# Modulation sums as rows, and latent-head outputs by token in halves of the array

## What is computed

```python
silu_c = jax.nn.silu(c)
silu_cc = jax.nn.silu(c_ctx)
m_lat = (silu_c @ w_ada[layer] + b_ada[layer])[:, None, :]
m_ctx = silu_cc @ w_ada[layer] + b_ada[layer]
sh1, sc1, g1, sh2, sc2, g2 = jnp.split(m_lat, N_MOD, axis=-1)
csh1, csc1, cg1, csh2, csc2, cg2 = jnp.split(m_ctx, N_MOD, axis=-1)
u_lat = _modulate(_rmsnorm(x, norm1_g[layer]), sh1, sc1)
u_ctx = _modulate(_rmsnorm(ctx, norm1_g[layer]), csh1, csc1)
```

```python
scores = jnp.einsum("bnihd,bnjhd->bnhij", qc * jnp.exp(a - a_mid), kc * jnp.exp(a_mid - a))
scores = jnp.where(tril, scores, 0.0)
o_intra = jnp.einsum("bnhij,bnjhe->bnihe", scores, vc)
o_inter = jnp.einsum("bnihd,bnhde->bnihe", qc * jnp.exp(a), s_start)
o = o * lax.rsqrt(jnp.mean(o * o, axis=-1, keepdims=True) + EPS) * gain
return o.reshape(bb, l, HG_WIDTH) * jax.nn.silu(g)
```

## Time and profile before

| | before |
|---|---|
| median of the runs, us | 2680.01 |
| the profiled execution's own time, us | 2679.24 |
| its span, us | 2677.4 |
| TensorE busy, share of the span | 99% |
| VectorE, ScalarE, POOL busy | 68%, 49%, 11% |
| mean granted TensorE clock | 0.998 |
| share of TensorE in the chain that ended last | 94% |
| read from HBM | 564.73 MB, 212 GB/s |

### The profile page before, as it was taken

One profiled execution on the slowest core, in us unless ns is written; L12 is line 12 of the kernel. 1 busy time (PEld: TensorE's weight loads), 2 busy tenths in 40 slices (PEclk: granted clock), 3 DMA queues, 4 the chain that ended last, 5 costly groups with the idle time before them and its releaser, 6 DMA issues.

```text
span 2677.4 us, 42752 instructions
## 1 busy us (share of the span) xinstructions
PE 2642.8 (99%) x18168; PEld 2414.4 (90%) x18168; DVE 1833.4 (68%) x2189; ACT 1323.8 (49%) x1746; POOL 281.4 (11%) x255
## 2 busy tenths in 40 slices
PE   9999999999999999999999999999999999999998
PEld 8888976998998989988999999998898898998997
DVE  5555665798999777787678866676555675445555
ACT  5455553554443443466874345666454444443443
POOL 1232321010000000010010311110000000000011
PEclk9999999999999999999999999999999999999999
DMA  9545454577777777795566744445657775555553
GB/s 308 171 156 158 146 175 143 195 262 269 271 260 285 269 284 282 283 338 176 157 233 243 266 134 150 136 151 194 219 170 251 266 282 196 190 177 196 188 179 124
DMA packets 289117, 571.28 MB, mean 213 GB/s; under 512 B 9702, under 2 KB 32513, under 8 KB 288608
## 3 DMA queue, kind: packets, MB, share of 16 engines
q1 hardware_dynamic: 283376, 548.69, 60.2%
q0 software_dynamic: 5552, 19.87, 2.5%
HBM read 564.73 MB, written 3.27 MB: 212 GB/s over the span
## 4 chain that ended last, share of the span: by engine, by line
PE 94%; DVE 3%; ACT 3%; issue 1%; POOL 0%; ACTq 0%; DVEq 0%; POOLq 0%
PE p_gemm L2110 49%; PE p_gemm L2159 32%; PE p_gemm L2136 3%; DVE w_lo L1232 1%; ACT w_hi L691 1%; PE p_b L2183 1%; PE p_b L2313 1%; PE p_b L2344 1%; PE p_b L2508 1%; PE p_b L2517 1%; PE p_b L2572 1%; PE p_b L2406 1%; PE p_gemm L2129 0%; PE p_b L2220 0%; PE p_b L2327 0%
## 5 line engine op out<-in xcount | busy, mean ns | idle before, releaser
L1232 DVE TENSOR_TENSOR w_lo<-w_raw,w_hi 128x1024 fp32r<-128x1024 f32 (+2 forms) x872 | 1068.5, 1229 | 729.7 <-ACT w_hi L691 728.5
L691 ACT ACTIVATE w_hi<-w_raw 128x1024 fp32r<-128x1024 f32 (+2 forms) x872 | 898.8, 1033 | 1226.4 <-PE p_gemm L2110 690.8
L2110 PE MATMUL p_gemm<-h_hi,w_hi 128*128 128x256 f32 x2928 | 831.5, 284 | 4.6 <-DVE w_lo L1232 2.5
L2110 PE MATMUL p_gemm<-h_lo,w_hi 128*128 128x256 f32 x2928 | 822.6, 281 | 0.0
L2110 PE MATMUL p_gemm<-h_hi,w_lo 128*128 128x256 f32 x2928 | 822.5, 281 | 0.0
L2110 PEld LDWEIGHTS p_gemm<-h_hi,w_hi 128*128 128x128 f32 x2928 | 551.7, 188 | 13.2 <-issue 7.1
L2110 PEld LDWEIGHTS p_gemm<-h_lo,w_hi 128*128 128x128 f32 x2928 | 551.9, 188 | 0.4
L2110 PEld LDWEIGHTS p_gemm<-h_hi,w_lo 128*128 128x128 f32 x2928 | 551.7, 188 | 0.0
L2159 PE MATMUL p_gemm<-w_hi,a_hi 128*128 128x512 f32 (+1 forms) x1056 | 406.1, 385 | 0.1
L2159 PE MATMUL p_gemm<-w_hi,a_lo 128*128 128x512 f32 (+1 forms) x1056 | 404.4, 383 | 0.0
L2159 PE MATMUL p_gemm<-w_lo,a_hi 128*128 128x512 f32 (+1 forms) x1056 | 404.2, 383 | 0.0
(11 more groups left out here) (402 smaller groups left out, 2483.2 us busy)
## 6 DMA issues: line engine op xcount, KB each, us to landing
w_raw<-in_w_mlp SPq DMA_DIRECT2D x124, 1024.0 KB, 5.2
w_raw<-in_w_in SPq DMA_DIRECT2D x107, 1024.0 KB, 5.3
ada_w<-in_w_ada SPq DMA_DIRECT2D x96, 1024.0 KB, 5.5
w_raw<-in_w_up SPq DMA_DIRECT2D x64, 1024.0 KB, 7.5
w_raw<-in_w_down SPq DMA_DIRECT2D x64, 1024.0 KB, 8.2
w_raw<-in_w_out SPq DMA_DIRECT2D x32, 1024.0 KB, 5.1
w_raw<-in_w_in SPq DMA_DIRECT2D x36, 768.0 KB, 4.7
cmp_w<-in_phi_w POOLq DMA_DIRECT2D x2, 2048.0 KB, 19.1
```

The source lines that it names most:

```text
L691: act.activation(WH[:, s % 4, :, 0:n], RAW[:, s // 2, 2 * (s % 2):2 * (s % 2) + 2, 0:n], ACT.Copy)\
L1232: dve.tensor_tensor(WL[:, s % 4, :, 0:n], RAW[:, s // 2, 2 * (s % 2):2 * (s % 2) + 2, 0:n], WH[:, s % 4, :, 0:n].bitcast(F32), ALU.subtrac ...
L2110: ins = pe.matmul(dst, w[:, s % 4, kk, cols], x[:, k, :], start=k == 0 and m % 2 == 0 and i == 0, stop=k == KC - 1 and i == 2, skip_group_ ...
```

## The change

It changes three things, and moves some steps for room.

**Sums as rows.** After the last step ScalarE rounds the 512 summed columns to `ADAT` and VectorE writes the remainder. TensorE, now after unit 3 (`ADA_AT`), multiplies a selector with them: 32 weight columns, of which one is ones, so that the total lands as row `i` of `PADA[0:32]` and zeros are added to the other rows. Three times (blocks 33, 57, 75) VectorE copies the 32 rows (`MODR`), TensorE turns them by four small transposes, and VectorE adds the bias as before. The last four totals, those of g2, have a full array of ones as weights; their row comes out on all partitions at once and VectorE adds it to the bias row in `G2B`. `ADA_BLOCKS` begins at 16 and skips 55.

**Outputs by token.** Weights and moving operand of the output products change places, so that the output is 128 tokens by 128 channels, twice. The sum of squares is then taken by ScalarE's accumulator along the row, the scale is one number per token (`HRS`), VectorE multiplies it in (`lat_scale`), and TensorE turns the result back (`lat_turn`) for `lat_out`.

**Halves of the array.** The scores are eight products of 64 x 64 on the diagonal instead of four of 128 x 128, and the inter-chunk products have 64 weight columns; both write partitions 0 to 63 or 64 to 127.

```diff
-ADA_AT = 2
-ADA_BLOCKS = [*range(17, 48), *range(55, 62), 72, 73, *range(80, 88)]
+ADA_AT = 3
+ADA_BLOCKS = [*range(16, 48), *range(56, 62), 72, 73, *range(80, 88)]
-MOD_READS = (13, 16, 20, 24)
+ADA_G2 = 20
+MOD_READS = (8, 16, 20)
+MOD_AT = (B_MLP1 + 17, B_HY + 1, B_WOUT2 + 3)
+MOD_ROWS = (0, 16, 24)
-C_SCALE = (13, 15, 19, 22)
-C_TURN = (14, 15, 16, 17, 20, 21, 23, 24)
+C_ROOT = B_MLP1 + 24
+C_SCALE = (0, 5, 11, 18)
+C_TURN = (1, 3, 7, 9, 13, 16, 20, 23)
-U_SCALE = (6, 11, 19, 29)
-U_TURN = (9, 14, 20, 25, 30, 36, 41, 46)
+U_SCALE = (6, 11, 19, 33)
+U_TURN = (12, 14, 20, 28, 36, 44, 52, 54)
...
+            def ada_top(b):
...
+                act.wait_ge(S("ada_summed"), 2 * UPB * (i + 1))
+                if i < ADA_CTX:
+                    act.activation(ADAT[:, 2, :], CTXA[:, i % 2, :], ACT.Copy)
+                act.activation(ADAT[:, 0, :], ADA[:, 1, 3, :], ACT.Copy).then_inc(S("ada_hi"), 1)
...
             def lat_square(h):
                 act.wait_ge(S("hg_o"), h + 1)
-                act.activation(OSQ[:, :], PB[1][:, 0:T], ACT.Square).then_inc(S("hg_osq"), 1)
+                for tb in range(2):
+                    ins = act.activation(OSQ[:, P * tb:P * tb + P], PB[1][:, P * tb:P * tb + P], ACT.Square, accum_out=HSS[:, tb:tb + 1])
+                ins.then_inc(S("hg_osq"), 1)
...
+                act.activation(HRS, HSS, ACT.Ln, bias=prm("eps"), scale=1.0 / P).then_inc(S("hg_oln"), 1)
...
+            def ada_rest(b):
...
+                dve.wait_ge(S("ada_hi"), i + 1)
+                if i < ADA_CTX:
+                    dve.tensor_tensor(CTXL[:, i % 2, :], CTXA[:, i % 2, :], ADAT[:, 2, :].bitcast(F32), ALU.subtract)
+                dve.tensor_tensor(ADAT[:, 1, :], ADA[:, 1, 3, :], ADAT[:, 0, :].bitcast(F32), ALU.subtract).then_inc(S("ada_lo"), 1)
+
             def ada_step(b, s):
+                if s == 1:
+                    ada_rest(b)
...
+            def lat_scale(h):
+
+                dve.wait_ge(S("hg_ors"), h + 1)
+                for tb in range(2):
+                    ins = dve.tensor_scalar(ON[:, tb, :], PB[1][:, P * tb:P * tb + P], HRS[:, tb:tb + 1], None, ALU.mult)
+                ins.then_inc(S("hg_out"), 1)
...
+                        if s == 3 and h > 0:
+                            lat_scale(h - 1)
                         if s == 4:
                             lat_keys(h)
-                        if s == 3 and h > 0:
+                        if s == 5 and h > 0:
                             lat_out(h - 1)
...
+                if s == 2:
+                    lat_scale(HG - 1)
                 if s == 3:
                     lat_out(HG - 1)
                     gated(0)
...
             clamp_gate(1)
+            slot(B_WOUT2, None, 0)
+            ada_step(B_WOUT2, 0)
             gated(1)
+            slot(B_WOUT2, None, 1)
+            ada_step(B_WOUT2, 1)
             mixed_lo(3)
...
+                pe.wait_ge(S("ada_lo"), i + 1)
+                halves = (ADAT[:, 0, :], ADAT[:, 1, :])
+                if i >= ADA_G2:
+                    ps = bank(i % 2, "mod_ready", i - ADA_G2 + 4)
+                    for n, w in enumerate(halves):
+                        ins = pe.matmul(ps[:, :], SEL[:, 31:32].to_broadcast([P, P]), w, start=n == 0, stop=n == 1)
+                else:
+                    rows = [(i if i < ADA_CTX else i + 8, halves)]
+                    if i < ADA_CTX:
+                        rows.append((i + 8, (ADAT[:, 2, :], CTXL[:, i % 2, :])))
+                    for row, ws in rows:
+                        for n, w in enumerate(ws):
+                            ins = pe.matmul(PADA[0:32, :], SEL[:, 31 - row:63 - row], w, start=i == 0 and row == 0 and n == 0, stop=True,
+                                            skip_group_check=True)
+                ins.then_inc(S("ada_used"), 1)
+
+            def modulation_turn(part):
+
+                pe.wait_ge(S("mod_rows"), part + 1)
+                ps = bank(0, "mod_ready", part + 1)
                 for m in range(4):
...
+                    ins = pe.transpose(ps[:, 32 * m:32 * m + 32], MODR[part][:, P * m:P * m + P], IDN[0:32, 0:32])
+                ins.then_inc(S("mod_turned"), 1)
...
                 for z in range(2):
-                    for i in range(2):
-                        ts = slice(P * i, P * i + P)
-                        ins = pe.matmul(PB[1][:, T * z + P * i:T * z + P * i + P], KM[:, z, ts], QM[:, z, ts], start=True, stop=True)
+                    for n in range(NCH):
+                        ts = slice(CHUNK * n, CHUNK * n + CHUNK)
+                        ins = pe.matmul(PB[1][CHUNK * (n % 2):CHUNK * (n % 2) + CHUNK, T * z + CHUNK * n:T * z + CHUNK * n + CHUNK],
+                                        KM[:, z, ts], QM[:, z, ts], start=True, stop=True)
...
+                bank(1, "hg_out", 2 * h + 1)
                 for z in range(2):
                     for i in range(2):
...
+                        pe.matmul(PB[1][:, P * i:P * i + P], SCT[:, z, i, :], HVN[:, i, :], start=z == 0 and i == 0, stop=False,
+                                  skip_group_check=True)
+                for i in range(NCH):
+                    for z in range(2):
                         n = i if z == 0 else NCH - 1 - i
                         state = start_state(h)[:, z, :] if i == 0 else ST[:, z, i - 1, :]
...
+                        rows = slice(CHUNK * (n % 2), CHUNK * (n % 2) + CHUNK)
+                        cols = slice(P * (n // 2), P * (n // 2) + P)
+                        ins = pe.matmul(PB[1][rows, cols], QAQ[:, z, CHUNK * n:CHUNK * n + CHUNK], state, start=False, stop=True,
+                                        skip_group_check=True)
...
+            def lat_turn(h):
+
+                ps = bank(1, "hg_out", 2 * h + 2)
+                for tb in range(2):
+                    ins = pe.transpose(ps[:, P * tb:P * tb + P], ON[:, tb, :], IDN[:, :])
+                ins.then_inc(S("hg_oturned"), 1)
...
-                        if s == 0 and h > 0:
-                            lat_square_sum(h - 1)
+                        if s == 4 and h > 0:
+                            lat_turn(h - 1)
...
-                if s == 0:
-                    lat_square_sum(HG - 1)
+                if s == 2:
+                    lat_turn(HG - 1)
...
-                        if g == 2 and q == 1 and s in G2_ROWS:
...
```

More of the change, by code:

```diff
@@ L254, in program @@
         CTXA = at("ada_ctx", A0 + 68 * K, [P, 2, 512])
+        CTXL = at("ada_ctx_lo", A0 + 68 * K, [P, 2, 512], F32R)
+        ADAT = at("ada_tops", 72 * K, [P, 3, 512], F32R)
+        SEL = at("row_select", A0 + 72 * K, [P, 64], F32R)
+        MODR = [at(f"mod_rows{i}", A0 + 68 * K if i == 0 else A0 if i == 1 else A0 + 64 * K, [32, 512]) for i in range(3)]
         CX = [at("ctx_x0", A0 + 64 * K, [P, 2, 512]), at("ctx_x1", A0 + 68 * K, [P, 2, 512])]
@@ L1698, in modulation, with gate_row @@
                 dve.sem_inc(S("mod_ready"), 1)
+            def gate_row(m):
+                row = G2B[:, 512 * m:512 * m + 512]
+                dve.wait_ge(S("ada_used"), ADA_G2 + m + 1)
+                dve.wait_ge(S("final_rows_loaded"), 32)
+                dve.tensor_tensor(row, row, PB[m % 2][:, :], ALU.add).then_inc(S("mod_ready"), 1)
             for g in range(GROUPS):
@@ L1847, in _ @@
                     ada_step(B_HY + i, s)
-                    if i == 1 and s == 4:
-                        modulation(1)
                     r = UPB * i + s
@@ L1970, in _ @@
                 for s in range(UPB):
+                    if m == 0 and s < 2:
+                        continue
                     if b < B_MLP2 - 1 or s < UPB - 1:
@@ L1973, in _ @@
                     ada_step(b, s)
-                    if m == 3 and s == 0:
-                        modulation(2)
                 dve.wait_ge(S("unit_used"), count(b + 1, None, UPB))
@@ L2054, in _ @@
                             rest_mod(6, s + 3, u2_half(s + 3), HL, HH)
-                        if g == 2 and q == 0 and s == 4:
-                            modulation(3)
                         if s == 1 and 1 <= q <= 4:
@@ L2446, in _ @@
                             ada_total(b)
+                        if b == MOD_AT[0] and s == 4:
+                            modulation_turn(0)
                         if g == GROUPS - 1 and UPB * (q - 4) + s in C_TURN:
@@ L2525, in _ @@
                         ada_total(b)
+                    if b == MOD_AT[1] and s == 4:
+                        modulation_turn(1)
                     r = UPB * (b - B_HY) + s
@@ L2618, in _ @@
                         ada_total(b)
+                    if b == MOD_AT[2] and s == 4:
+                        modulation_turn(2)
                     if s == 2:
```

186 lines of the change are left out of this document (93 added, 93 removed).

## The result

Six runs of the changed kernel have a median of 2689.76 us (2687.46 to 2695.36), six of the kernel before 2680.8. The ratio is 1.0033 with a 95% interval of 1.0022 to 1.0044. The forecast was 2688.3, slower.

The account below looks back on a forecast made before the run. It took TensorE's in-order queue, busy 99% of the span, as the bound. Gains of 25.5 and losses of 33.8 took 2679.2 to 2687.5, plus 0.8 for the runs' median 2688.3 us; range 2669 to 2698, to hold 8 in 10.

Parts of the forecast that it names:

- totals: 24 modulation totals as 512-column products, 0.216 each plus 0.3 for changing shape with 32 weight columns: 8.9 us gained.
- slow products: TensorE possibly slow after block 71's wait, 0 to 2.2 us, taken as 2 lost; nothing after the waits of 2.8.
- context heads: Blocks 49 to 55: most of the waits for `hg_ke` go, 4.5 us gained; net 4.4 after 1.0 lost in block 48.
- outputs in halves, scores: Eight latent heads: inter-chunk products in overlapping halves gain 4.4 us; scores shorter by some 0.3 a head gain 0.
- gates, block 72: The wait of 2.57 us for `lo` of unit 4 goes, since slots 0 and 1 move ahead: 2.6 gained.
- waits for totals, blocks 18, 20, 28: Context stage: VectorE behind by 2.5 to 3 us, so TensorE waits 1 to 1.5 each: 3 lost.
- waits for totals, blocks 48, 60: Block 56's total, now in block 48, waits for VectorE, late with the residual: 1.0 us lost; block 60 not forecast.
- seven waits in 64 to 70: `lat_turn` waits for `lat_scale`, behind two `lo` on VectorE: 2.8 us a head, seven times, 19.6 lost.
- block 71: Last latent head: `lat_turn` after unit 2 waits for a scaling behind ScalarE's Ln and Exp pairs: 7.1 us lost.
- Rival 1: Latent heads' new waits don't come, VectorE reaching `lat_scale` in time: 2659.6 us, chance 0.10; middle form about 2678, 0.10.
- rival 3: VectorE bounds the context stage, its lead of 3.6 us eaten; totals give nothing there: up to 8, 2696, chance 0.09.
- rival 2: Halves don't overlap in the latent heads' inter-chunk products: 0.85 us a head, 6.8 in all, 2695, chance 0.08.

Follow-up runs that it names:

- e5: The kernel of e4 with the total of block 60 back after unit 3; 2655.38 us, ratio to the kernel before 0.9897.
- e1: The changed kernel with `lat_scale` right behind the decays on VectorE, ahead of two remainders, in blocks 64 to 70; 2667.19 us, ratio to the kernel before 0.9953.
- e2: The changed kernel with block 71 alone reordered on ScalarE, VectorE and TensorE, two table loads fewer; 2679.95 us, ratio to the kernel before 0.9998.
- e7: e6 with a latent head's masks and states ahead of the remainder of s = 6 on VectorE, not s = 7; 2646.26 us, 0.9865 of the kernel before.
- e3: The changed kernel with two totals later on TensorE, block 48 after unit 6, block 60 after unit 5; 2690.89 us, ratio to the kernel before 1.0038.
- e8: e5 with all sixteen inter-chunk products of a latent head on one half of the array, part of the computation left out; 2662.69 us, one run.
- e9: e6 with the score products of the kernel before, four of 128x128; blocks 64 to 70 take 28.32 to 28.35 us each, as in e6.
- e10: e7 with the score products of the kernel before; blocks 64 to 70 take 28.07 to 28.28 us each, e7 27.65 to 27.84.
- e4: The changed kernel with the edits of e1, e2 and e3 together; 2660.04 us, ratio to the kernel before 0.9924.
- e6: e5 with `lat_out` ahead of the remainder of s = 5 on VectorE; 2651.64 us, ratio to the kernel before 0.9884.

## Why the prediction was right, step by step

The time was right to 1.5 us, and that is in part luck, since errors of both signs met: the totals gave 5.0 more than forecast, 3.0 of waits in the context stage didn't come and 2.3 of waits for remainders went, against 7.5 more of slow products and 4.7 more of waits in blocks 48 and 60. A restart in the table is what TensorE loses behind a wait beside the wait itself: two transposes take 0.21 without a wait and 3.02 with one of 2.59, so 0.2.

| step | forecast | measured | from |
|---|---|---|---|
| totals | +8.9 | +13.9 | 28.8 in all before, 15.0 after |
| g2 spread | +3.6 | +3.6 | eight groups cost 7.2 before, four 3.6 after |
| context heads | +5.4 | +5.0 | `hg_ke` waits 4.8 to 0.6 |
| square sum to transposes | +1.6 | +1.7 | 0.42 to 0.21 (e5, no wait) |
| outputs in halves, scores | +4.4, 0 | +4.5 | both groups, 40.1 to 35.6 |
| gates, block 72 | +2.6 | +2.85 | 25.56 to 22.71 |
| modulation turns | -2.1 | -1.7 | 0.56 each |
| waits for totals, blocks 18, 20, 28 | -3 | 0 | least lead 0.6 |
| waits for totals, blocks 48, 60 | -1.0 | -5.7 | 4.42 and 0.95, with the restart |
| `lo` waits of block 48, covered | 0 | +2.3 | three before, none after |
| seven waits in 64 to 70 | -19.6 | -19.7 | 18.1 and seven restarts of 0.23 |
| block 71 | -7.1 | -7.3 | 7.08 and a restart |
| slow products (half clock) | -2 | -9.5 | 2.5, 1.5 and four of 1.2 to 1.5 |

The measured column sums to 10.0 lost where the profiled times differ by 9.2; the rest I can't place.

**The waits.** This step held to the tenth: a head's delay, counted from start to start, was put at 2.8 and is 2.60 of wait and about 0.2 of restart. It could be, since each term came from a row and nothing upstream of VectorE changed. e1 shows that the place of one step on VectorE is the whole of it in blocks 64 to 70, and e2 that the order of ScalarE and VectorE is nearly all of it in block 71. Rival 1 fell: VectorE reached `lat_scale` when the earlier trace rows said.

**The slow products.** Here a step failed. The prediction gave the waits of 2.8 nothing, since the one wait of 2.57 had normal spacing behind it, and it held that no wait between the first and the last big product was long enough. The trace of before had a second case, which I hadn't looked at, near the kernel's start:

```profile
77.08 0.31 PE L2286 MATMUL p_b<-ident,proj 40*128 40x40 f32 x2 [2.39 <-DVE proj L1417]
77.33 0.80 PE L2136 MATMUL p_gemm<-w_hi,h_hi 128*128 128x512 f32 x1
77.92 0.63 PE L2136 MATMUL p_gemm<-w_lo,h_hi 128*128 128x512 f32 x1
78.35 0.63 PE L2136 MATMUL p_gemm<-w_hi,h_lo 128*128 128x512 f32 x1
```

The starts are 0.43 apart and not 0.233, for 3.2 us, 1.5 lost. Two windows (as above) show the clock there, in the kernel before and in e2:

```profile
77.00:81.00 4.00, 3.92 (x11) 3.16 (x12) 3.52 (x7) 0.65 (x1) 0.12 (x1) 0.57 1.02 200
11.00:18.00 7.00, 4.87 (x27) 4.64 (x27) 6.42 (x10) 5.70 (x10) 0.00 (x0) 0.76 1.06 390
```

This wait is in all twelve kernels profiled, and that early all run nearly the same instructions. It took 2.4 to 2.6 in ten of them, with slow products behind it in five (before, after, e1, e5, e7) and none in the other five (e2, e3, e8, e9, e10). These other five are the ones that had a slow stretch of some 3.4 us at the start of their first block instead, the second window, and the first five had none there. Ahead of the first block TensorE stood 2.1 us in all, in one or two waits, in each of the ten. In the five with the slow stretch 0.8 to 1.7 of that stood directly before the first big product, in the others 0.6 or less. So it hangs on more than the length of a single wait; on what, these runs don't show.

Where the wait near 77 took 3.2 and 4.7 (e4, e6) slow products came. Of the seven waits of 2.6 it was 4, 4 and 5 (after, e2, e3). The waits of 4.4 and 7.1, profiled three times each, and the two of 4.0 in block 61 (e3, e4), were followed by 1.3 to 2.5 of loss each time. Those of 1.0 to 1.2 in e1, e4, e5 and e8 never were, in 28 cases, nor was the one of 2.16 in block 49 of before or the one of 1.6 at the start of block 76 in all twelve. So the term should have been about half of the seven, 5, and with the earlier trace rows beside the rows above it could have been. The Trainium skill, "TensorE: Matmul & The Clock Gate", Part 1, has an idle array fall to 1.2 GHz and come back with work. The trace agrees: 0.213 between starts of 256 columns, and 0.50 in the clock's column. That it hits the same wait in one run and not in the next is also the likely reason why six runs of the kernel after spread over 7.9 us. The mean granted clock of each run speaks for it: 0.991 in the two slowest of the six and 0.993 in the other four; 0.996 in the fastest of the ten runs of e2 (2676.63) and 0.992 in the slowest (2686.62); and 0.997 to 0.998 in the four of e7, which have few such waits and spread over 2.5 us. Most of these runs have no trace, so it isn't shown wait by wait.

**The totals.** The size was off: each new product was right (0.23, forecast 0.216), but the 0.3 for changing shape isn't there. I had taken it from the earlier trace rows, where the products in the strip are short themselves. The output products of e7 and e8 are short too, and some 0.35 stands beside them. The totals' products move 512 columns each, and it vanishes whether their neighbours move 512 or 256. Which property of the long products hides it wasn't tried. The Trainium skill, "TensorEngine Tiling (Array Packing)", Key Properties, says that a change of the tiling mode drains TensorE. No total here shows a cost of it; whether the 0.35 beside the short products is that cost isn't shown. The rule of the Trainium skill, "TensorEngine Tiling (Array Packing)", Instruction Overhead, that a product with one moving column takes as long as one with 60, would have made this part a loss, of 14 by the prediction's own terms (20 for the new totals less 6) and not of the 11 that it states. The trace disagrees: the part gave 13.9.

**The context stage.** The waits of 3 didn't come. In block 20, VectorE and TensorE:

```profile
590.64 0.68 DVE L1280 TENSOR_TENSOR ada_ctx_lo<-ada_ctx,ada_tops 128x512 fp32r<-128x512 f32 x1
591.24 0.68 DVE L1281 TENSOR_TENSOR ada_tops<-ada_w,ada_tops 128x512 fp32r<-128x512 f32 x1
...
592.52 0.85 PE L2266 MATMUL p_b<-ada_tops,row_select 128*32 128x512 f32 x3
```

The remainder ends 0.6 before the product that needs it. That is the least lead of the eight (0.8 in block 28, 1.2 in 18 and 26, 1.9 where VectorE is on time). So VectorE is behind by 1.3 there and not by 2.5 to 3, and rival 3 falls, though it is a near miss: it is busy 98% to 100% of blocks 25 to 29.

**Block 48.** This step failed too, in its size. I had put this wait at 1.0, and two rows of the kernel before, had I set them side by side, gave it. There the `lo` of s = 1 ends at 1239.2, behind the first pieces of the residual; with the total's remainder behind it 1239.8. TensorE ends unit 3 at 1235.3. That is 4.5 (measured 4.42). I had walked through block 65 in this way and not through block 48. What it costs net is less, 3.9 where the wait, its restart and the slow products are 6.1: the three waits for remainders of before went under it, and e3 and e5 show them come back (2.5).

**The scores.** The step that said "shorter products gain nothing here, the wait behind them grows" is shown by e6, e7, e9 and e10. Without the wait they gain 0.44, where the prediction had 0.3 (scores and updates took 1.96 before and take 1.67 after). The other 0.15 isn't placed: put back into e10, the old scores and the updates take 2.1 to 2.3.

**The halves.** e8 shows the overlap: without it a head takes 0.86 more, which is the 0.85 that rival 2 gave for its absence. The Trainium skill, "TensorEngine Tiling (Array Packing)", Key Properties, says that different tiles run in parallel, and the trace agrees, for fp32 products of 64 weight columns, with that 0.86.

## What to carry to other kernels

Where TensorE is the bound and its queue is in order, a change that makes its work cheaper is judged by the first instruction of it that waits: 34 us of cheaper work and of waits taken away lost to 42 of ten new waits and of what followed them. Before a step is moved, walk the block row by row for every queue that it enters and every buffer that it gives back, since moving the total by two units in block 60 cost 5. In these runs a wait of 2.4 us or more on TensorE cost 1.2 to 2.5 more than itself in over half of the cases, so where a step can stand early on the engine that is waited for, it is put there.

## What I had not expected of the hardware

- Waits of 2.4 to 2.6 us of TensorE in the middle of its work are followed by 2.8 to 3.4 us of products at half the clock (once over 6) in some executions and not in others, for the same instructions, in 18 of 32 cases. It costs 1.2 to 1.6 each, in one case over 2. It begins at once or up to 1.5 us after the wait has ended. Waits of 1.0 to 1.2 had none in 28 cases.
- The column of the granted clock shows these stretches (0.50 over 3.4 us, 0.95 over the 32 of the block, 0.57 from 77 to 81), but not the kernel's first one, from 1.6 to 5.5 us.
- A product of 512 columns with 32 weight columns between products with 128 costs 0.23, as much as one of 512 with 128 does, with no charge for the change.
- Two remainders of VectorE in a row take 1.7 to 1.9 each and not 1.2 in blocks 64 to 70 while GpSimd works beside it (3.43 for two, with GpSimd at `hg_ke` from 1707.40); whether GpSimd is the cause wasn't tried.
